# Loop entry in another order, three-expert rounds last, and second weights of ranked experts issued by ScalarE on a queue of its own

## What is computed

```python
x = x + g_m * mixer(h, ...)
h = rms_norm(x, norm_ffn_g[l]) * (1.0 + sc_f) + sh_f
x = x + g_f * moe_ffn(h, w_router[l], b_router[l], w1[l], w3[l], w2[l], ws1[l], ws3[l], ws2[l])
# moe_ffn: sigmoid scores, 4 of 8 groups of experts, top 8 of 64 experts for each token, weights
# normalised; out = (silu(x w1) * (x w3)) w2 for each expert, and one shared expert for all tokens
```

## Time and profile before

| what | value |
|---|---|
| median of 3 runs (range) | 2012.62 us (2004.08 to 2015.46) |
| the profiled execution: its time, its span | 2008.7 us, 2006.8 us |
| PE busy | 1819.2 us (91%) |
| DVE, ACT busy | 915.9 us (46%), 360.7 us (18%) |
| DMA moved | 586.38 MB, mean 292 GB/s |

### The profile page before, as it was taken

How to read it: one execution, slowest core, us unless ns; L and a number is a source line. 1 busy time by engine, 2 the same in 40 slices (tenths; PEclk the granted TensorE clock), 3 DMA queues, 4 the chain that set the end, 5 groups by cost and what they waited for, 6 DMA issues and landing times. The chain is left out here.

```text
span 2006.8 us, 27853 instructions
## 1 busy us (share of the span) xinstructions
PE 1819.2 (91%) x10492; PEld 1043.2 (52%) x10492; DVE 915.9 (46%) x2058; ACT 360.7 (18%) x701; POOL 55.0 (3%) x166
## 2 busy tenths in 40 slices
PE   5999999989879878889999989888788787999998
PEld 3847884443433334376588644333333333585485
DVE  2897532543433433369874253433433423451351
ACT  2143112011111111123231011111111112141131
POOL 1000002000000000000000010000000001010000
PEclk9999999999989989999999999989989988998998
DMA  9655637899999999957455449999999998333430
GB/s 348 205 215 184 235 126 282 340 421 420 421 421 420 420 420 421 409 179 218 168 215 203 190 169 419 421 421 420 420 421 420 421 420 239 109 116 109 155 105 21
DMA packets 146471, 586.38 MB, mean 292 GB/s; under 512 B 12844, under 2 KB 17568, under 8 KB 96416
## 3 DMA queue, kind: packets, MB, share of 16 engines
q1 hardware_dynamic: 144928, 581.47, 74.5%
q0 software_dynamic: 1408, 3.10, 0.6%
HBM read 583.49 MB, written 1.05 MB: 291 GB/s over the span
## 5 line engine op out<-in xcount | busy, mean ns | idle before, releaser
L1385 PE MATMUL banks<-weight_ring,x_units 128*32 128x512 f32 x2560 | 418.3, 637 | 0.2 <-DMA weight_ring<-in_w 0.2
L1385 PE MATMUL banks<-spare_slot,x_units 128*32 128x512 f32 x768 | 221.0, 740 | 96.3 <-DMA weight_ring<-in_w 96.3
L2163 DVE TENSOR_TENSOR sig_h<-banks,sig_h 128x256 f32<-128x256 f32 x52 | 22.1, 425 | 413.6 <-ACT sig_h L1672 413.6
L1385 PEld LDWEIGHTS banks<-spare_slot,x_units 128*32 128x32 f32 x768 | 58.2, 132 | 255.3 <-issue 255.3
L1385 PEld LDWEIGHTS banks<-weight_ring,x_units 128*32 128x32 f32 x2560 | 109.9, 117 | 131.9 <-issue 131.2
L1043 PE MATMUL banks<-h_t,weight_ring 128*128 128x256 f32 x768 | 170.1, 380 | 0.0
L1043 PEld LDWEIGHTS banks<-h_t,weight_ring 128*128 128x128 f32 x768 | 145.3, 190 | 21.3 <-issue 1.6
L2442 PE MATMUL banks<-weight_ring,h_t 128*128 128x512 f32 (+2 forms) x384 | 134.1, 509 | 0.5 <-DMA weight_ring<-in_w_in 0.5
L983 PE MATMUL banks<-h_t,weight_ring 128*128 128x256 f32 x512 | 113.9, 385 | 3.7 <-DVEq L1740 3.7
L1409 PE MATMUL banks<-qk,conv 128*32 128x512 f32 x448 | 94.3, 594 | 22.0 <-issue 22.0
L1422 PE MATMUL banks<-o_parts,slot_of 128*128 128x512 f32 x416 | 110.6, 406 | 3.1 <-DVE o_parts L2200 3.1
(11 more groups left out here) (509 smaller groups left out, 2413.5 us busy)
## 6 DMA issues: line engine op xcount, KB each, us to landing
weight_ring<-in_w SPq DMA_DIRECT2D x208, 1024.0 KB, 17.4
weight_ring<-in_w_in SPq DMA_DIRECT2D x36, 2048.0 KB, 12.8
slots<-in_w SPq DMA_DIRECT2D x52, 1024.0 KB, 20.7
weight_ring<-in_w_mod SPq DMA_DIRECT2D x24, 2048.0 KB, 12.4
spare_slot<-in_w SPq DMA_DIRECT2D x48, 1024.0 KB, 11.2
qk<-in_w SPq DMA_DIRECT2D x26, 1024.0 KB, 21.4
h_t<-in_w SPq DMA_DIRECT2D x26, 1024.0 KB, 14.0
qk_t<-in_w SPq DMA_DIRECT2D x24, 1024.0 KB, 14.7
```

What stands on the lines that cost most here:

```text
L1385: mm = nc.tensor.matmul(h_bank[own, :], x_blk[:, i, k, own], w13(p % RING_X)[:, :, k, :], start=(k == 0), stop=(k == KT - 1), skip_group_c ...
L2163: v.tensor_tensor(act_pair, h_bank[:, 0:FF], sig_pair, ALU.mult)
```

## The change

- **Rounds.** The three-expert rounds are now 3, 5, 7, ... 25; round 2, round 4 and the even ones hold two. The last round holds three experts.
- **SP at the entry.** Next-layer parameters are loaded much earlier (behind the chunk `("gt", 1, 0)`); second weights of experts 0 and 1 right behind `("wo", 1)`, ahead of the shared ws2. First weights of 0 to 2 and second weights of 2 follow as before. Expert 3 is no longer waited for ahead of `table_ready`: SP waits for `table_ready`, issues first weights of 4, then waits for `sh_h_done` and issues first and second weights of 3.
- **Second weights of ranked experts** are issued by ACT (`second_weights(n)`) in round n, behind the sigmoid of round n: those whose slot was freed by round n-1; that of expert 4 in round 2, behind `sh_done`.
- **TensorE at the entry.** `mod("rt")` comes behind `rt` and behind the arrival of the shared weights; the eight k-steps of the shared first product of half 0 are split 5, 2, 1; two steps of half 1 come behind the list's products, and `over` behind them. The turn of the shared activations moves from ahead of round 0 to behind its first product, the shared second product from round 0 to round 1.
- **VectorE.** Some steps of the choice are merged or dropped, `mod(14)` goes behind `one_hot_b(0)`, the count of passes behind `one_hot(0)`, and `slot_weights(0)` behind all four `block_x`.

```diff
@@ round_plan
-        if n < 2 or (n % 2 and n > 5):
+        if n in (2, 4):
+            kind = (0, 0, 0, 1)
+        elif n % 2 == 0 or n < 2:
             kind = (0, 0, 1, 1)
-        elif n % 2 == 0:
+        else:
             kind = (0, 0, 1, 2)
-        else:
-            kind = (0, 0, 0, 1)
@@ SP, load_rest
                         expert13(l, e, p % RING_X)
-                        if held is not None:
-                            load_second(at, held, p - 1)
-                        held = e
-                    load_second(at, held, N_EXPERTS - 1)
+                        if p == FORMED and first:
+
+                            sp.wait_ge(sh_h_done.sem, sh_h_done.at(l, T))
+                            expert13(l, 3, 3)
+                            expert2(l, 3, 3)
@@ ScalarE
+                    def second_weights(n):
+
+                        freed = [p for p in range(RING_X, N_EXPERTS) if LAST_ROUND[p - RING_X] == n - 1]
+                        if n == 2:
+
+                            act.wait_ge(sh_done, at(T, T))
+                            act.sem_inc(wait_carrier, 1)
+                            freed = [FORMED] + freed
+                        for p in freed:
+                            if p - RING_X == min(PLAN[n - 1]):
+                                act.wait_ge(o_done, at(2 * NR, 2 * n))
+                                act.sem_inc(wait_carrier, 1)
+                            e = act.value_load(K.table[0:1, FIRST_COL[p]:FIRST_COL[p] + 1], min_val=0, max_val=N_EXPERTS - 1)
+                            nc.scalar.dma_start(w2_slots[p % RING_X].rearrange("p f n -> p (f n)"),
+                                                A["w2"][ds(l, 1), ds(e, 1)].rearrange("a b (p f) n -> p (a b f n)", f=2))\
+                                .then_inc(w2_filled[p % RING_X], 16)
@@ ScalarE, one_pass
                         sigmoid(n)
+                        if n > 0:
+                            second_weights(n)
@@ TensorE, entry
-                shared_h(0, range(KT))
+                moe_y_free(1, 0)
+                if l + 1 < DEPTH:
+                    mod("rt")
+                shared_h(0, range(0, 5))
...
-                moe_free(3)
-                shared_h(1, range(0, 1))
+                shared_h(0, range(5, 7))
...
-                shared_h(1, range(1, 2))
-
+                shared_h(0, range(7, 8))
+
+                moe_y_free(0, 0)
...
+                moe_free(3)
+                shared_h(1, range(0, 2))
@@ TensorE, one_pass
                         if n == 0:
+                            pe.wait_ge(act_cleared, at(1, 1))
+                            pe.wait_ge(weight_ready, at(TURNS, 1))
+                            for t in range(T):
+                                shared_turn(t)
+                            pe.wait_ge(sh_act_t_ready, at(T, T))
+                        if n == 1:
                             pe.wait_ge(shared2_gated.sem, shared2_gated.at(l))
                             for t in range(T):
                                 shared_second(t)
```

More of the change, by code:

```diff
@@ L443, in _groups_1 @@
         + [("wo", h, t) for t in range(T) for h in range(2)] + mod_groups("wo", layer)
-        + [("xT", 1, g) for g in range(4)] + mod_groups("turned", layer) + ["rt_halves"] + mod_groups("rt", layer) + ["rt"]
+        + [("xT", 1, g) for g in range(4)] + mod_groups("turned", layer) + ["rt_halves", "rt"] + mod_groups("rt", layer)
         + [("=moe_y", t, h) for t in range(T) for h in range(2)] + ["-moe_h", "-moe_x"] + [("-moe_o", h) for h in range(2)]
@@ L845, in _ @@
                                 .then_inc(gate_loaded.sem, 16)
[L847 removed]
+                for e in range(FORMED - 1):
                     before = loads[l][len(loads[l]) - RING + e][3]
[L849 to L852 removed]
+                    if before[0] == "mod_dve":
                         sp.wait_ge(dve_parts.sem, dve_parts.at(l, before[1] - DVE_CHUNKS[0] + 1))
@@ L1308, in _ @@
                 mm.then_inc(cols_done.sem, 1)
-                pe.wait_ge(over_ready.sem, over_ready.at(l))
-                nc.tensor.matmul(o_bank[:, at_over:at_over + PASSES - 1], K.ones[e64, :], over[e64, :], start=True, stop=True)
                 for t in range(T):
@@ L1313, in _ @@
                                      start=True, stop=True)
-                nc.tensor.matmul(o_bank[:, 0:COLS], K.part[e64, 0:1].to_broadcast([N_EXPERTS, P]), to_col[e64, :], start=True,
-                                 stop=True).then_inc(list_done.sem, 1)
+                nc.tensor.matmul(o_bank[:, 0:COLS], K.part[e64, 0:1].to_broadcast([N_EXPERTS, P]), to_col[e64, :], start=True, stop=True)
+                moe_free(3)
+                shared_h(1, range(0, 2))
+                pe.wait_ge(over_ready.sem, over_ready.at(l))
+                nc.tensor.matmul(o_bank[:, at_over:at_over + PASSES - 1], K.ones[e64, :], over[e64, :], start=True, stop=True)\
+                    .then_inc(list_done.sem, 1)
                 shared_h(1, range(2, KT))
+                moe_y_free(0, 1)
+                moe_y_free(1, 1)
                 moe_free(1)
@@ L1429, in one_pass @@
                     gather(0, 1)
-                    pe.wait_ge(act_cleared, at(1, 1))
-                    for t in range(T):
-                        shared_turn(t)
                     for q in (2, 3):
@@ L1690, in move_held @@
                         nc.scalar.activation(x_blk[:, 1, 0:KT // 2, :], x_held, ACT.Copy).then_inc(x_moved, 1)
-                    for t in range(T):
-                        act.wait_ge(sh_turned, at(T, t + 1))
-                        nc.scalar.activation(act_t[:, t], sh_turned_at[t].rearrange("p (f n) -> p f n", f=2), ACT.Copy)\
-                            .then_inc(sh_act_t_ready, 1)
                     for n in range(NR):
@@ L1701, in one_pass @@
                         sigmoid(n)
+                        if n > 0:
+                            second_weights(n)
+                        if n == 0:
+                            for t in range(T):
+                                act.wait_ge(sh_turned, at(T, t + 1))
+                                nc.scalar.activation(act_t[:, t], sh_turned_at[t].rearrange("p (f n) -> p f n", f=2), ACT.Copy)\
+                                    .then_inc(sh_act_t_ready, 1)
                         if i > 0 and it + 1 < TURNS:
@@ L2080, in _ @@
                 dve.drain().then_inc(to_col_ready.sem, 1)
-                v.tensor_reduce(n_tiles[:], to_col[:], AX.X, ALU.add)
-                dve.drain()
-                v.tensor_scalar(over[:], K.pass_slots[:], n_tiles[:], count[:], ALU.mult, ALU.is_lt)
-                dve.drain().then_inc(over_ready.sem, 1)
                 def shared_act(t):
@@ L2116, in _ @@
                 one_hot(0)
+                v.tensor_reduce(n_tiles[:], to_col[:], AX.X, ALU.add)
+                dve.drain()
+                v.tensor_scalar(over[:], K.pass_slots[:], n_tiles[:], count[:], ALU.mult, ALU.is_lt)
+                dve.drain().then_inc(over_ready.sem, 1)
                 dve.wait_ge(list_done.sem, list_done.at(l))
@@ L2201, in o_split @@
                                 .then_inc(o_ready, 1)
-                    block_x(0, 0)
-                    block_x(0, 1)
+                    for q in range(4):
+                        block_x(0, q)
                     slot_weights(0, first=True)
-                    block_x(0, 2)
-                    block_x(0, 3)
                     for n in range(NR):
```

99 lines of the change are left out of this document (44 added, 55 removed).

## The result

The changed kernel took 2046.33 us (median of 4 runs, 2038.76 to 2053.06); the kernel before, run beside it, 2008.35 (2001.21 to 2015.46). The ratio is 1.0191, with a 95% interval from 1.0153 to 1.0229: 38 us slower. The span of the profiled execution is 2040.2 us against 2006.8, +33.4. 2032 was predicted, 24 more than the profiled execution before.

A forecast was written before the change was run, and what follows sets the result against it. The expert loops were taken as bound by weight transfers. Layer 0's 6.0 + 1.5 + 4 = 11.5 and layer 1's 6.5 + 1.5 + 4 = 12, on the profiled 2008.7 us, gave 2032; 8 in 10 from 1999 to 2055.

The forecast's parts named there:

- (c): Whole kernel: the forecast's own case, 2018 to 2045 us, chance 0.55.
- rival (d): Three-expert rounds: uneven queues or late ACT issues run the queue dry, 1 to 2 us a pair; 2045 to 2070; chance 0.15.
- part 1: Entry of the weight stream: 9 us ahead in layer 0, about 6 in layer 1, if every gain went through.
- the cover that I had taken as whole: Layer 0 entry: loads moved up cost nothing; without spare queue room, two second weights hold back modulation weights by 5.0 us.
- part 2: Rounds 0 to 2: ring slots allow at most 24 MiB by the end of round 2's first product, so early streaming gains nothing.
- E: End of a layer's last weight landing, 843.9 before in layer 0; forecast at least 849.9 and 1670.2.
- h2: End of round 2's first product, 420.06 before in layer 0; forecast 426.0 and 1246.3.
- part 3: Round 0 starts +4 us later in layer 0, +2.6 in layer 1; round 2's first product ends 2.0 later still.
- The signs named for layer 1: Layer 1 trace: round 2's first product ends at about 1246, the last weights land at about 1672.
- part 4: Round 2: TensorE stalls 2 to 5 us for expert 4's second weights; 1.5 us a layer reach the last landing.
- No holes later: Later rounds: a backlog stays in the queues, cost 0, up to 5 us a layer if ACT's issues come late.
- part 5: Round 25: its first product waits, then takes 9.6 us; +4 us a layer, bounds -2 and +8.

The follow-up runs named there:

- `sp_entry`: Kernel before with the new order of rounds on one queue, plus only SyncE's side of the changed entry; 2010.1 us, ratio 1.0005.
- `entry_queue_end`: `queue_o_done_end` with SyncE's side of the changed entry added; 2005.0 us, ratio 0.9983.
- `compute_split_undone`: `compute_entry` with all eight k-steps of the shared product's first half ahead of the count again, instead of five; 2018.2 us, ratio 1.0058.
- `queue_only`: Kernel before with only the ranked experts' second weights moved to ScalarE's queue, behind its sigmoid; 2023.2 us, ratio 1.0074.
- `queue_o_done`: Kernel before with the new order of rounds and second weights on ScalarE's queue, issued ahead of its sigmoid; 2020.0 us, ratio 1.0059.
- `queue_o_done_end`: `queue_o_done` with ScalarE issuing behind its sigmoid again in the last two rounds; 2010.0 us, ratio 1.0010.
- `compute_entry`: Kernel before with the new order of rounds on one queue, plus only the engines' side of the changed entry; 2018.4 us, ratio 1.0052.
- `after_o_done`: Changed kernel with ScalarE's second-weight issues ahead of its sigmoid of the same round instead of behind it; 2033.6 us, ratio 1.0110.

## Why the prediction was right, and where it was off

The sign, the range and the places were right; the size was 24 us for a measured 38. The median of 2046.3 lies 1 us above the prediction's own branch (c), 2018 to 2045 with 0.55, and so at the lower edge of rival (d)'s; the profiled execution (2041.9) is in (c). From part to part:

**The early stream pays nothing (part 1).** Right, and shown alone by `sp_entry`. Two details were off: expert 4's first weights were issued at 376.4, not near 372, since `over` and with it the table came later; and the loads moved up were not wholly free. Shared weights landed at 354.8 instead of 351.8, behind two second weights, and TensorE waited 4.6 us for them. In the kernels with that part alone (`sp_entry`, `entry_queue_end`) round 0 started at 380.3 and 376.6, inside the 376.4 to 379.5 of those without it or just over, so their price stays open. In `sp_entry` TensorE waited 2.2 us for the modulation weights of `mod("rt")`, the cover that I had taken as whole; in `entry_queue_end` it did not.

**The ring cap (part 2).** Right as a mechanism: the queues stood empty up to the end of first product 2, bytes flowed again behind it, and E = h2 + 423.9 would be 853.4; it was 861.7. In layer 1 it would be 1690.7 and was 1703.5. The 8.3 us of layer 0 are the second hole (5.1 us, share 0.36 over 8 us), and a sum of small ones: 419 GB/s for 420 over 394 us is 0.9, and the next stage's first load, which SP issued at 843.98, shared the engines with the last three second weights; on one queue it stood behind them. That load's share, some 2 us, is what the others leave; no run isolates it.

**h2 (part 3).** From the start of round 0 to h2 were 44.8 us in both layers for 45.6. The start of round 0 itself was off: +8.3 for +4 in layer 0, and in layer 1 356.8 us behind the loop of layer 0 instead of 352.3, +4.4 for +2.6. (The signs named for layer 1, 1246 and 1672, leave out layer 0's own delay; with its 11.5 us they are 1257.8 and 1683.5, for a measured 1266.8 and 1703.5.) Of the 8.3, some 3 are scatter: with the engines' entry of before the eight profiles have 376.4 to 380.3 (mean 377.9), with the changed one six have 380.8 to 384.9 (383.3), which is +5.4. In layer 1 the step that failed, by the rows of `compute_split_undone`, is that VectorE's list stays ahead of TensorE: `over` came late.

**Second weights late (part 4).** This term was the most under-sized. TensorE's stall in round 2 was 6.2 us (2 to 5 expected), and its second product took 5.4 us for 3.6, as its matmuls took 1.07 us each at first, at a granted clock of 0.50 (440 to 444), and 0.60 at the end of it. I let 1.5 us a layer reach E; the hole behind it was 5.1 us in layer 0, and in layer 1 the slice from 1270 to 1300 has 350 GB/s, 5 us. "No holes later" was wrong, too: 411 GB/s over 430 us in layer 1 is 9 us, of which that hole is 5; the 4 that are left are inside the 5 that I had allowed for late issues. `queue_only` shows the same without the cap. I counted that 7 or 8 MiB are issued at each first product's end and last until the next one, but not that with two queues the second weights of a round are in before the last of its first weights, so that less is left behind a first product that has waited. That was near rival (d), with 0.15: in `queue_only` the steady part lost 6.6 and 6.3 us over some 9 pairs of rounds a layer, and in the changed kernel, at 419 and 417 GB/s in the same stretches, 1.6 and 2.4 us.

**The end (part 5).** It started at E - 5.9 and E - 5.4 for E - 3.8 and took 9.3 and 9.7 us for 9.6: near enough, and inside its bounds. The Trainium skill's page DMA: Bandwidth & Descriptors, section Queues, rings and completion order, has engines take turns between filled queues; the pair `queue_o_done` and `queue_o_done_end` agrees: three second weights beside them put off the last first weights by 4.1 us. The same page of the Trainium skill, section Issuing engines are not separate DMA queues, says that several issuers bring no bandwidth; the traces agree (421 GB/s with one queue, and 421 with two where both had enough to do).

**The sum.** The parts up to the end of layer 1's loop were predicted at 23.5 and measured at 42; the profile of before had 9 us of low clock behind the loops. By single parts in the runs: new plan 0 (about 2 us a layer in the profile), SP's entry 0 to 2, engines' entry 12, queue 28 us, together 40 to 42 for the 38 measured. The undoing of the queue alone left 10 us, and 10 and 28 make the 38 by construction; that the engines' entry is most of the 10 rests on `compute_entry` and `sp_entry`.

## What to carry to other kernels

In a loop bound by weight transfers through a ring, count at each end of a consumer step which bytes may be under way: an earlier start of the stream is worth nothing if the slots for it come free later, and a load moved to a later event takes its bytes out of that count. Here a second DMA queue added no bandwidth and took away the order of need; if one is used, keep loads that are needed later out of the time in which the critical ones are under way, and look for what the next stage issues on the other queue. When a trial that cures a cause shows nothing, look in its trace for what it made worse: the earlier issue was worth 10 us once the last two rounds were left out of it. And when a mean rate falls, look at it in stretches of a few us before calling the engines slower.

## What was not expected of the hardware

- Two queues moved 412 to 420 GB/s over hundreds of microseconds, where one moved 420 to 421, and the difference was not a slower rate: between the holes they moved 421 (600 to 650 us of `queue_only`). With the earlier issue the means were 419 and 420 (`after_o_done`, from 480 to 825 and from 1310 to 1640), with two queues as before.
- After a wait of 6 us the matmuls of a second product took 1.07 us each, at first, instead of 0.60, at a granted clock of 0.50; twelve matmuls of the shared product behind a pause of 1.8 us took 7.11 us at a mean clock of 0.76, instead of 5.42 at 1.00 without one.
- Identical code had round 0 of layer 0 start anywhere from 376.4 to 379.5 us, and the stretch behind the loops took 332 to 345 us, with a granted clock of 1.00 to 0.92 in its last 210 us. A single profile can't tell a part of 3 us at layer 0's entry, nor one of 10 us behind the loops. The stretch between the two loops repeated within 0.3 us in six of the eight kernels with the engines' entry of before (352.1 to 352.3), and was 355.1 in the other two (`queue_only`, `queue_o_done_end`), for no reason that I found.
